# Inverses of unit triangular matrices held as 64x64 blocks under each other instead of 128x128 matrices with two blocks on the diagonal

## The reference, cut to what matters

```
for each head and each chunk of 64 tokens:
    N = strictly triangular part of (products of the chunk's vectors), 64 x 64
    U = inverse(I - N) @ (right-hand side)     # then the state is updated with U
```

## Time and profile before

| | us |
|---|---|
| median of 3 runs | 3771.29 |
| lowest and highest run | 3769.44, 3778.99 |
| the profiled execution | 3777.16 |
| its span in the trace | 3775.4 |
| PE busy in the span | 3331.5 (88%) |
| DVE, ACT, POOL busy | 2298.6, 1328.7, 618.3 |

### The profile page before, as it was taken

One profiled execution on the slowest core, in us unless ns is written; L12 is line 12 of the kernel. 1 busy time (PEld: TensorE's weight loads), 2 busy tenths in 40 slices (PEclk: granted clock), 3 DMA queues, 4 the chain that ended last, 5 costly groups with the idle time before them and its releaser, 6 DMA issues. The chain is left out here.

```text
span 3775.4 us, 43307 instructions
## 1 busy us (share of the span) xinstructions
PE 3331.5 (88%) x16964; PEld 2698.2 (71%) x16964; DVE 2298.6 (61%) x3581; ACT 1328.7 (35%) x1874; POOL 618.3 (16%) x540
## 2 busy tenths in 40 slices
PE   8987779998987788998975887789999898899998
PEld 7864568876864567886745786767778787677787
DVE  7888647985778647994647564554442433744434
ACT  2224525762234524773212012222222314722222
POOL 0035310000035300001404241301100102511000
PEclk8987789999986788999987887889999999999999
DMA  7620006982520005991220000002222221122222
GB/s 277 254 86 1 6 12 252 375 342 76 217 76 1 9 12 212 375 354 51 89 73 1 1 1 1 1 19 99 84 94 90 89 90 50 38 98 80 91 97 78
DMA packets 59578, 401.33 MB, mean 106 GB/s; under 512 B 6768, under 2 KB 8432, under 8 KB 12272
## 3 DMA queue, kind: packets, MB, share of 16 engines
q1 hardware_dynamic: 53616, 356.62, 25.6%
q0 software_dynamic: 5760, 41.95, 3.0%
HBM read 396.45 MB, written 2.10 MB: 106 GB/s over the span
## 5 line engine op out<-in xcount | busy, mean ns | idle before, releaser
L135 PE MATMUL ps<-t_part,weight_hi 128*128 128x512 f32 x2152 | 864.2, 402 | 70.2 <-DVE scr_part L180 38.7
L137 PE MATMUL ps<-t_part,ring_lo 128*128 128x512 f32 x2152 | 849.9, 395 | 0.0
L136 PE MATMUL ps<-scr_part,weight_hi 128*128 128x512 f32 x1640 | 649.5, 396 | 0.0
L135 PEld LDWEIGHTS ps<-t_part,weight_hi 128*128 128x128 f32 x2152 | 413.0, 192 | 165.0 <-DVE ring_lo L167 70.0
L345 DVE TENSOR_TENSOR ring_lo<-ring,weight_hi 128x2048 fp32r<-128x2048 f32 x133 | 313.2, 2355 | 341.1 <-ACT weight_hi L338 341.1
L338 ACT CAST weight_hi<-ring 128x2048 fp32r<-128x2048 f32 x133 | 253.8, 1908 | 669.7 <-PE ps L137 669.7
L137 PEld LDWEIGHTS ps<-t_part,ring_lo 128*128 128x128 f32 x2152 | 411.5, 191 | 87.8
L136 PEld LDWEIGHTS ps<-scr_part,weight_hi 128*128 128x128 f32 x1640 | 316.0, 193 | 70.2 <-issue 5.1
L136 PE MATMUL ps<-big_part,weight_hi 128*128 128x512 f32 x512 | 200.7, 392 | 0.0
L201 POOL TENSOR_TENSOR big<-big 128x512 f32<-128x512 f32 x28 | 47.5, 1696 | 892.5 <-ACT big L194 888.7
L3035 DVE SCALAR_TENSOR_TENSOR big<-ps,rstd 128x512 f32<-128x512 f32 x64 | 44.2, 690 | 164.1 <-PE ps L137 164.0
(11 more groups left out here) (618 smaller groups left out, 7179.5 us busy)
## 6 DMA issues: line engine op xcount, KB each, us to landing
ring<-in_w_moe SPq DMA_DIRECT2D x84, 1024.0 KB, 5.0
t<-in_w_moe SPq DMA_DIRECT2D x84, 1024.0 KB, 5.0
ring<-in_w SPq DMA_DIRECT2D x64, 1024.0 KB, 4.8
t<-in_w_ada POOLq DMA_DIRECT2D x40, 1024.0 KB, 6.6
ring<-in_w_in SPq DMA_DIRECT2D x32, 1024.0 KB, 5.7
ring<-in_even_in SPq DMA_DIRECT2D x15, 1024.0 KB, 4.9
ring<-in_qkv SPq DMA_DIRECT2D x12, 1024.0 KB, 4.9
ring<-in_w_out SPq DMA_DIRECT2D x8, 1024.0 KB, 4.8
```

The lines of the kernel that those rows point to most:

```text
L135: pe.matmul(bank, w_hi, x_hi, start=first, stop=False)
L136: pe.matmul(bank, w_hi, x_lo, start=False, stop=False)
L137: return pe.matmul(bank, w_lo, x_hi, start=False, stop=last)
```

## The change

All five kinds of tile become 128x256: a 64x64 block of an even chunk lies in partitions 0 to 63, the block of the odd chunk beside it in partitions 64 to 127 under it, and the zero quarters are no longer held or computed. Each product of 128x128 by 128x128 becomes two products of 64x64 by 64x64, one in rows and columns 0 to 63 of TensorE, one in rows and columns 64 to 127, issued in turns (`HALVES`), both into one PSUM bank, in partitions 0 to 63 and 64 to 127. POOL's masks, ACT's copies and DVE's sums in the stage run over 256 columns instead of 512. The number of items, the semaphores and the order are the same; the convolution's taps, sigmoids and products are unchanged.

Where `NT` is written, one DVE instruction over 128x512 becomes two over 64x256 (one for each half of the partitions). In the scans the product with `TT` takes 64 rows instead of 128. The masks are packed two to a 128x128 tile, and `K.tri` has 8 tiles instead of 10.

```diff
+HALVES = (slice(0, 64), slice(64, 128))
...
-    bank = lambda i: K.ps[:, i, :].rearrange("p (i c) -> p i c", c=P)
-    identity = K.ident[:, :].unsqueeze(1).to_broadcast([P, 4, P])
+    bank = lambda i: K.ps[:, i, 0:256].rearrange("p (i c) -> p i c", c=64)
+    identity = K.tri[:, 7:8, 0:64].to_broadcast([P, 4, 64])
+    level = lambda n: K.tri[:, 4 + n // 2:5 + n // 2, 64 * (n % 2):64 * (n % 2) + 64].to_broadcast([P, 4, 64])
...
-            g.tensor_tensor(NO(n), NT(b), K.tri[:, 4 + lev:5 + lev, :].to_broadcast([P, 4, P]), ALU.mult).then_inc(off.up(), 1)
+            g.tensor_tensor(NO(n), NT(b), level(lev), ALU.mult).then_inc(off.up(), 1)
...
             for i in range(4):
-                ins = pe.matmul(bank(n % 2)[:, i, :], NO(n)[:, i, :], T(b)[:, i, :], start=True, stop=True)
+                for r in HALVES:
+                    ins = pe.matmul(bank(n % 2)[r, i, :], NO(n)[r, i, :], T(b)[r, i, :], start=True, stop=True)
...
                 if lev < 5:
-                    pe.matmul(bank(2 + n % 2)[:, i, :], TT(b)[:, i, :], X(b)[:, i, :], start=True, stop=True)
-                ins = pe.matmul(bank(4 + n % 2)[:, i, :], X(b)[:, i, :], TT(b)[:, i, :], start=True, stop=True)
+                    for r in HALVES:
+                        pe.matmul(bank(2 + n % 2)[r, i, :], TT(b)[r, i, :], X(b)[r, i, :], start=True, stop=True)
+                for r in HALVES:
+                    ins = pe.matmul(bank(4 + n % 2)[r, i, :], X(b)[r, i, :], TT(b)[r, i, :], start=True, stop=True)
...
             for i in range(4):
-                ins = pe.matmul(bank(b % 2)[:, i, :], NO(b)[:, i, :], K.ident[:, :], start=True, stop=True)
+                for r in HALVES:
+                    ins = pe.matmul(bank(b % 2)[r, i, :], NO(b)[r, i, :], K.ident[r, r], start=True, stop=True)
...
+    pairs = lambda buf, at: (lambda b: buf[:, at + b * 256:at + (b + 1) * 256].rearrange("p (i c) -> p i c", c=64))
+    NT, T, TT, X = pairs(K.T1, 0), pairs(K.T1, 2048), pairs(K.scr, 0), pairs(K.scr, 2048)
+    NO = lambda n: pairs(K.scr, 6144)(n % 2)
...
+    def keep_pairs(v, j, b, bank):
+        for r in HALVES:
+            mask = K.tri[r, 2:3, r].unsqueeze(1).to_broadcast([64, 2, 2, 64])
+            ins = v.tensor_tensor(NT(b)[r].rearrange("p (h i) c -> p h i c", h=2), bank[r, :, :, r], mask, ALU.mult)
+            if r is HALVES[0]:
+                ins.then_inc(st.up(), 1)
+        return ins
...
-                    ins = pe.matmul(K.ps[r, 4 + p, in_bank(i)], TT(t)[:, place(i), r], Z[:, i * 64:(i + 1) * 64],
+                    ins = pe.matmul(K.ps[r, 4 + p, in_bank(i)], TT(t)[r, place(i), :], Z[r, i * 64:(i + 1) * 64],
...
-            v.tensor_tensor(NT(h), bank(3), F, ALU.mult).then_inc(st.up(), 1)
+            for r in HALVES:
+                v.tensor_tensor(NT(h)[r], bank(3)[r, :, r], F[r, :, r], ALU.mult).then_inc(st.up(), 1)
...
-                    ins = pe.matmul(K.ps[r, 2 + g, in_bank(h)], TT(h)[:, t, r], Z[:, hd(h)], start=True, stop=True)
+                    ins = pe.matmul(K.ps[r, 2 + g, in_bank(h)], TT(h)[r, t, :], Z[r, hd(h)], start=True, stop=True)
...
-    K.tri = K.sb("tri", [P, 10, P])
+    K.tri = K.sb("tri", [P, 8, P])
```

## The result

| | before | after |
|---|---|---|
| median, us | 3772.08 | 3748.47 |
| lowest and highest of 7 runs | 3769.21, 3778.99 | 3731.23, 3750.91 |
| profiled execution, span | 3777.16, 3775.4 | 3745.20, 3743.4 |
| mean granted clock | 0.908 | 0.896 |

The ratio is 0.9922 [0.9909, 0.9935]: faster, by 24 us where 69 were forecast, and outside the range of 3686 to 3732. The instructions are 46199 instead of 43307.

A forecast was written before the change was run, and what follows sets the result against it. TensorE alone set the pace of the inverse items before; afterwards DVE would bound the RWKV runs. Savings of 75.6 us, less 1.6 for `NT` and 5 for the clock, gave 69: 3702 against 3771, range 3686 to 3732.

The forecast's parts named there:

- TensorE's pace: Inverse stages' items: both quarters work fully at once, so a pair of 64-wide records costs 0.060 us.
- Rival 2: Inverse items: TensorE can't be fed instructions fast enough; gain only 16 us, 3755, or half way 45, 3726; chance 0.10.
- rival 4: Inverse items: the quarters take turns because of the shared PSUM bank or the array; items 54 us, time 3771; chance 0.04.
- 5: Rival: each MATMUL has a fixed price of 0.064 us that doesn't shrink; 7 to 10 us slower, 3780; chance 0.03.
- The rival on the clock (3): Inverse items: the half-used array lets the clock fall to 0.50; gain 3 to 5 us, 3767; chance 0.05.
- The items: The 20 items of each inverse run: 27.9 us in GDN, set by TensorE; 32.3 in RWKV, set by DVE.
- The loss from a clock that rises later: Start of the inverse items: part runs at half pace, 1.5 to 2 us a run, 5 in all, bounds 0 and 12.
- rival 1: RWKV inverse runs: DVE's taps meet POOL's masks nearly every time, DVE 37 us; gain 57, 3714; chance 0.14.
- its sign: RWKV inverse runs: DVE busy almost throughout, and TensorE's idle time before `both` ended by two named DVE lines.
- Opening and end: Inverse runs: opening until the first `join` 5.9 us instead of 10.0 to 10.7; RWKV end 3.3 instead of 3.6.
- `NT`: Stages writing `NT`: two DVE instructions over 256 columns instead of one over 512, 12 times; 1.6 us added.
- The scans: RWKV and GDN scans: the product with `TT` in half the rows disturbs nothing; 0 us, bounds -2 to +5.

The follow-up runs named there:

- the later run: The changed kernel itself, with no further edit, measured again beside the follow-up kernels: 3750.60 us, 0.9936 times the kernel before.

## Why the prediction was wrong

- **TensorE's pace.** Forecast 0.060 for a pair of records, measured 0.058, sustained through whole items. Rivals 2, 4 and 5 fall, and 3 as well: the clock stays at 1.00 in the items once it is there. Of rival 4: L1588 and L1590 write one PSUM bank from both row halves in each pair, and the pairs lie 0.058 apart. The Trainium skill's rule (TensorEngine Tiling, "Restrictions and Gotchas") is contradicted by this, for two row halves that write different partitions of the bank. Rival 2's doubt, the feeding, is settled too: four MATMULs and four loads in 0.116 us are 0.0145 us an instruction.
- **The items.** Forecast 27.9 us for GDN, measured 29.6; for RWKV 32.3, measured 33.1. The loss from a clock that rises later was forecast at 1.5 to 2 a run, 5 us in all. In GDN's run the first 4.9 us of the items are at 0.50 (the first line below), which costs half of that, 2.4, where TensorE sets the pace; without it the items would have taken 27.2, so the forecast for them was good to 0.7. In the first RWKV run the first 5.8 us are at 0.50, and from there on DVE is busy for 26.85 of 27.3 us, TensorE for 25.2 (the second line): DVE bounds this part, as forecast. Its busy time was forecast at 30.8 and was 28.1, and POOL's masks, taken at 0.61 us, took 0.85; rival 1, with DVE at 37, did not come. TensorE's few waits in these items (1.9 us) are put down to POOL, ACT and the last update of the opening, and not to L1629 or L1630, as the prediction had it for its sign.

```profile
2348.70:2353.60 4.90, 4.83 (x91) 4.86 (x93) 0.75 (x2) 1.00 (x3) 2.39 (x4) 0.50 0.02 3
```
```profile
2053.20:2080.50 27.30, 25.23 (x797) 23.89 (x794) 26.85 (x51) 9.58 (x22) 18.33 (x19) 1.00 0.02 4
```

- **Opening and end.** Openings forecast at 5.9 us: 2041.73 to 2047.61, 5.9. Ends 3.3, measured 3.6.
- **The inverses in sum.** 75.6 less 5 for the clock, 70.6 forecast; 71.9 measured.
- **`NT`.** 1.6 forecast; measured 0.8 and 0.4 in the two `rwkv_ab` and 1.9 in `gdn_pairs`, 3.1 in sum. In `gdn_pairs` the clock was 0.59 instead of 0.61; how much of the 1.9 is due to that is not shown.
- **The scans: the step that failed.** "L2542 has the same number of records and columns, only half the rows, [...] so nothing runs that it could disturb: 0, bounds -2 to +5." As durations this was right: L2714 takes 1.97 us either way. But it was priced as an instruction and not by what it does to the clock. Measured: +6.9 and +3.1 in and behind the second RWKV scan, +27.5 in GDN's, 37.5 in sum, against an upper bound of 5. (The bounds were put on 32 chunk steps; three scans of 8 chunks have 24.) That the scans might be longer than now stood among the signs of being wrong, with no price and no chance. The rival on the clock (3) was looked for in the stage that was rewritten, where both quarters are busy and the clock stayed at 1.00 once up, and not in the neighbour, where half of a product was taken away with nothing in its place. The earlier trace rows could not show what a window over GDN's scan of the kernel before would have: the stage starts at 0.50 and spends its first 8 us there, so that the rise in it was worth 27 us and was not certain.

```profile
2446.40:2454.60 8.20, 5.43 (x24) 4.75 (x25) 4.36 (x10) 0.00 (x0) 0.00 (x0) 0.50 0.00 0
```
```profile
2454.60:2497.80 43.20, 37.75 (x298) 32.90 (x297) 25.30 (x77) 0.00 (x0) 0.00 (x0) 1.00 0.00 1
```

With that one part taken back the time is 3708 to 3714, and 0.9831 times 3772 is 3708: with the scans left in 128 rows, the forecast of 3702 would have held within its range.

What stays open: why the changed kernel has runs at 3731 beside those at 3745 to 3751. The two traces that there are (3745.20, and that of the later run) have GDN's scan at 0.50 throughout; in the runs at 3731 the clock may have risen late in it, which no trace shows.

## What to carry to other kernels

A change that takes work from TensorE without making any instruction shorter (half the rows of a product, zeros left out) saves nothing and can cost much, if the stage begins at 1.2 GHz: look at each stage that the change touches for the granted clock at its start and where it rises, and price the case that it doesn't, at the stage's whole length. Where zeros cost nothing in duration, as here (1.97 us with 64 rows and with 128), leave them in. Where such a loss is there, try products at the head of the stage: 24 of them bought 26 us here. Where the clock rose by itself, 6 at the head of each scan bought nothing that could be told from the noise.

## What the runs showed of the hardware

- Two products in opposite quarters of TensorE (rows and columns 0 to 63, rows and columns 64 to 127) run fully side by side: 0.058 us for a pair of 64-column fp32 records, also into one PSUM bank, where one such record over 128 rows and one half of the output took 0.060 in the scan.
- The profile's busy share does not show the trouble: TensorE counts as busy for 72.9 of 78.8 us in the GDN scan at 1.2 GHz, and for 42.9 of 51.6 in the one at 2.4. From 2400 to 2420 us of the changed kernel it counts as busy for all 20.0 us, and the clock stays at 0.50.
- The same stretch of work can stay at 1.2 GHz for 79 us or at 2.4 GHz to its end, and a product in 64 or in 128 rows, or 24 products ahead of it, decides which (78.8 us at 0.50 against 51.6 at 0.92).
